# Suffix sums of a stick-breaking attention: fp32 products against fp32r products of a rounded part and an exact rest

## What is computed

```python
def block(args):
    qb, start = args
    z = jnp.einsum('bhqd,bhkd->bhqk', qb, k).astype(f32) * scale
    qpos = start + jnp.arange(Q_BLOCK)
    mask = kpos[None, :] < qpos[:, None]
    log_beta = jax.nn.log_sigmoid(z)
    log_1m = jnp.where(mask, jax.nn.log_sigmoid(-z), 0.0)
    between = lax.cumsum(log_1m, axis=3, reverse=True) - log_1m
    a = jnp.where(mask, jnp.exp(log_beta + between), 0.0)
    return jnp.einsum('bhqk,bhkd->bhqd', a.astype(v.dtype), v)
```

## Time and profile before

| | |
|---|---|
| three runs | 1589.37, 1589.56, 1590.39 us, median 1589.56 |
| profiled execution, first to last instruction (its span) | 1588.8 us |
| TensorE (PE) busy | 1560.3 us, 98% |
| weight loads (PEld), beside the products | 1402.7 us, 88% |
| VectorE (DVE) busy | 983.1 us, 62% |
| ScalarE (ACT) busy | 821.1 us, 52% |
| GpSimd (POOL) busy | 149.2 us, 9% |
| data moved | 309.40 MB |

### The profile page before, as it was taken

How to read it: one execution, slowest core, us unless ns; L and a number is a source line. 1 busy time by engine, 2 the same in 40 slices (tenths; PEclk the granted TensorE clock), 3 DMA queues, 4 the chain that set the end, 5 groups by cost and what they waited for, 6 DMA issues and landing times.

```text
span 1588.8 us, 25389 instructions
## 1 busy us (share of the span) xinstructions
PE 1560.3 (98%) x10689; PEld 1402.7 (88%) x10689; DVE 983.1 (62%) x1614; ACT 821.1 (52%) x1204; POOL 149.2 (9%) x140
## 2 busy tenths in 40 slices
PE   7999999999999999999999999999999999999997
PEld 6888999988989899997899999889888888889986
DVE  5786744446566664554765667568747866664554
ACT  4586544444579754453454564444545546364442
POOL 2220011000002101011001100001000000001000
PEclk9999999999999999999999999999999999999999
DMA  9766757766563476777555577599673565585552
GB/s 328 260 210 227 232 193 229 253 241 226 172 204 107 159 230 200 229 251 244 188 186 186 186 159 194 178 189 175 145 156 70 135 161 184 171 279 193 194 186 80
DMA packets 224418, 309.40 MB, mean 195 GB/s; under 512 B 5005, under 2 KB 146721, under 8 KB 224305
## 3 DMA queue, kind: packets, MB, share of 16 engines
q1 hardware_dynamic: 222208, 301.48, 62.3%
q0 software_dynamic: 1664, 5.84, 1.1%
q10 hardware_dynamic: 432, 0.45, 0.1%
HBM read 306.71 MB, written 1.05 MB: 194 GB/s over the span
## 4 chain that ended last, share of the span: by engine, by line
PE 88%; DVE 5%; ACT 5%; issue 1%; DMA 1%; POOL 0%; DVEq 0%; ACTq 0%
PE ps L137 86%; PE ps L140 3%; DVE wl L150 2%; ACT SA L146 1%; ACT L146 1%; ACT wh L146 1%; DVE SM L160 1%; ACT SA L147 1%; DMA raw<-in_a_w_qkv_dram 0%; DMA X<-in_x_dram 0%; DVE SA L160 0%; DVE X L160 0%; DVE FT L150 0%; DVE SM L157 0%; ACT OA L146 0%
## 5 line engine op out<-in xcount | busy, mean ns | idle before, releaser
L150 DVE TENSOR_TENSOR wl<-raw,wh 128x1024 fp32r<-128x1024 f32 x498 | 606.8, 1258 | 396.2 <-ACT wh L146 395.6
L146 ACT ACTIVATE wh<-raw 128x1024 fp32r<-128x1024 f32 x498 | 501.9, 1054 | 233.0 <-PE ps L137 117.0
L137 PE MATMUL ps<-XPf,wh 128*128 128x256 f32 x1408 | 242.6, 278 | 0.0
L137 PEld LDWEIGHTS ps<-XPf,wh 128*128 128x128 f32 x1408 | 212.7, 188 | 4.3 <-issue 4.2
L137 PE MATMUL ps<-XPf,wl 128*128 128x256 f32 x704 | 195.1, 277 | 0.0
L137 PE MATMUL ps<-XPc,wh 128*128 128x256 f32 x832 | 145.0, 279 | 0.0
L137 PE MATMUL ps<-wh,HTH 128*128 128x512 f32 x352 | 137.8, 392 | 0.0
L137 PE MATMUL ps<-wh,HTL 128*128 128x512 f32 x352 | 137.2, 390 | 0.0
L137 PE MATMUL ps<-wl,HTH 128*128 128x512 f32 x352 | 137.2, 390 | 0.0
L137 PEld LDWEIGHTS ps<-XPf,wl 128*128 128x128 f32 x704 | 132.3, 188 | 0.0
L137 PEld LDWEIGHTS ps<-XPc,wh 128*128 128x128 f32 x832 | 125.9, 188 | 1.2 <-issue 1.0
(11 more groups left out here) (350 smaller groups left out, 2704.0 us busy)
## 6 DMA issues: line engine op xcount, KB each, us to landing
raw<-in_w_ffn_in_dram SPq DMA_DIRECT2D x66, 1024.0 KB, 5.2
raw<-in_ffn_w_gate_up_dram SPq DMA_DIRECT2D x44, 1024.0 KB, 5.6
raw<-in_w_in_dram SPq DMA_DIRECT2D x40, 1024.0 KB, 8.6
raw<-in_w_ada_dram SPq DMA_DIRECT2D x36, 1024.0 KB, 5.2
raw<-in_w_ffn_out_dram SPq DMA_DIRECT2D x30, 1024.0 KB, 5.0
raw<-in_ffn_w_down_dram SPq DMA_DIRECT2D x20, 1024.0 KB, 5.1
raw<-in_a_w_qkv_dram SPq DMA_DIRECT2D x12, 1024.0 KB, 7.5
raw<-in_kv_w_dram SPq DMA_DIRECT2D x8, 1024.0 KB, 5.4
```

What stands on the lines that cost most here:

```text
L137: return NOTHING if self.e is None else self.e.matmul(o, l, r, start=start, stop=stop, skip_group_check=skip)
L146: return self.e.activation(o, i, fn, bias=bias, scale=scale)
L150: return NOTHING if self.e is None else self.e.tensor_tensor(o, a, b, f)
```

## The change

Phase 1 splits P, as the dense layers split their weights, and multiplies the parts as fp32r. ACT rounds P to fp32r (`high_parts`) into the free tile `SA[2*hd%8]`, seen there as `SAR[2*hd%8]`; DVE takes P minus it (`low_parts`) over P itself, `SAR[2*hd%8+1]`. TensorE multiplies constant by high part (384 columns, and 128 with `neg`), waits for the low part, and does the same with it. The constants stand as fp32r in `NEG` (written once, over a buffer `MT` that is free at that time). `high_parts` stands first in ACT's tick, `low_parts` first in DVE's, so both parts of a pair are made in the very tick in which TensorE multiplies them. The exponential of phase 1 no longer waits for DVE's "bp".

```diff
@@ -238,6 +238,7 @@
         C = fixed("C", [P, CK])
         SM = fixed("SM", [P, 208])
         MT = [fixed(f"MT{i}", [P, 512]) for i in range(2)]
+        NEG = at("NEG", [P, 2, P], fixed.o - 4096, F32R)
         FT = [fixed(f"FT{i}", [P, 512]) for i in range(2)]
         at0 = fixed.o
         AT = fixed("AT", [P, 512])
@@ -258,7 +259,9 @@
         kT = a_("kT", [P, 8, T])
         VA = a_("VA", [P, 2, D])
         OA = a_("OA", [P, 2, D])
+        sa0 = a_.o
         SA = [a_(f"SA{i}", [P, 384]) for i in range(8)]
+        SAR = [at(f"SAR{i}", [P, 384], sa0 + 1536 * i, F32R) for i in range(8)]
         TA = [SG[0], a_("TA1", [P, 384])]
         LV = at("LV", [P, 256], r0)
 
@@ -703,12 +706,15 @@
                     S, P_ = SA[2 * hd % 8], SA[2 * hd % 8 + 1]
                     if phase == 1:
                         o = ps("bs", hd)
-                        pe.wait_ge(*v_att.at("bm", hd))
-                        pe.wait_ge(*g_att.at("bm", hd))
-                        pe.mm(o[:, 0:256], con("ngt"), P_[:, 0:256], False, False, True)
-                        pe.mm(o[:, 128:256], con("neg"), P_[:, 256:384], False, True, True)
-                        pe.mm(o[:, 256:384], con("ngt"), P_[:, 256:384], False, True, True).then_inc(
-                            *scored.up("bb", hd))
+                        ngt, neg = NEG[:, 0, :], NEG[:, 1, :]
+                        high, low = SAR[2 * hd % 8], SAR[2 * hd % 8 + 1]
+                        pe.wait_ge(*a_small.at("neg"))
+                        pe.wait_ge(*a_att.at("bh", hd))
+                        pe.mm(o[:, 0:384], ngt, high[:, 0:384], False, False, True)
+                        pe.mm(o[:, 128:256], neg, high[:, 256:384], False, False, True)
+                        pe.wait_ge(*v_att.at("bl", hd))
+                        pe.mm(o[:, 0:384], ngt, low[:, 0:384], False, False, True)
+                        pe.mm(o[:, 128:256], neg, low[:, 256:384], False, True, True).then_inc(*scored.up("bb", hd))
                         give(("bs", hd), a_att, "ba", hd)
                 if phase == 2:
                     g, c0 = p // 2, T * (p % 2)
@@ -1362,7 +1368,6 @@
                     S = SA[2 * hd % 8]
                     if phase == 1:
                         act.wait_ge(*scored.at("bb", hd))
-                        act.wait_ge(*v_att.at("bp", hd))
                         act.act(S[:, :], ps("bs", hd)[:, 0:384], ACT.Exp).then_inc(*a_att.up("ba", hd))
                 if phase == 2 and p % 2:
                     g, H = p // 2, head("ho")
@@ -1375,6 +1380,12 @@
                     if g == 1:
                         act.wait_ge(*a_att.at("bo", 0))
                         act.act(H[:, 0:2, :], two(OA[:, 0, 0:512]), ACT.Copy).then_inc(*a_turned.up("ho", 0))
+
+            def high_parts(p):
+                for hd in (2 * p, 2 * p + 1):
+                    act.wait_ge(*v_att.at("bm", hd))
+                    act.wait_ge(*g_att.at("bm", hd))
+                    act.act(SAR[2 * hd % 8][:, :], SA[2 * hd % 8 + 1][:, :], ACT.Copy).then_inc(*a_att.up("bh", hd))
 
             def logarithms(p):
                 for hd in (2 * p, 2 * p + 1):
@@ -1521,10 +1532,15 @@
                         m = act.act(head("hq")[:, k, :], qT[:, k, :], ACT.Copy, 0.0, gain("mix_pre_g", 8)(k))
                     m.then_inc(*a_turned.up("hq", kp))
                 yield
+                act.act(NEG[:, :, :].rearrange("p a b -> p (a b)"), C[:, CC["ngt"][0]:CC["ngt"][0] + 2 * P], ACT.Copy
+                        ).then_inc(*a_small.up("neg"))
                 tick = iter(B_TICKS)
                 for step in B_STEPS:
                     if step == "t":
                         heads = next(tick)
+                        for p, phase in heads:
+                            if phase == 1:
+                                high_parts(p)
                         for p, phase in heads:
                             attention_b(p, phase)
                         for p, phase in heads:
@@ -1999,6 +2015,13 @@
                         dve.wait_ge(*a_att.at("ba", hd))
                         dve.tt(S[:, 0:128], S[:, 0:128], con("mlt"), ALU.mult).then_inc(*v_att.up("bw", hd))
 
+            def low_parts(p):
+                for hd in (2 * p, 2 * p + 1):
+                    i = 2 * hd % 8
+                    dve.wait_ge(*a_att.at("bh", hd))
+                    dve.wait_ge(*g_att.at("bm", hd))
+                    dve.tt(SAR[i + 1][:, :], SA[i + 1][:, :], SAR[i][:, :].bitcast(F32), ALU.subtract).then_inc(*v_att.up("bl", hd))
+
             def sizes(p):
                 for hd in (2 * p, 2 * p + 1):
                     dve.wait_ge(*scored.at("bs", hd))
@@ -2214,6 +2237,9 @@
                     if step == "t":
                         parts = next(tick)
                         for p, phase in parts:
+                            if phase == 1:
+                                low_parts(p)
+                        for p, phase in parts:
                             if phase == 0:
                                 sizes(p)
                         for p, phase in sorted(parts, key=lambda u: -u[1]):
```

## The result

| | before | after |
|---|---|---|
| median of four runs each | 1589.97 us | 1610.63 us |
| lowest to highest | 1589.37 to 1591.72 | 1610.11 to 1611.28 |
| ratio | | 1.0126, interval 1.0113 to 1.0140 |
| span of the profiled execution | 1588.8 us | 1609.5 us |
| mean granted clock of TensorE | 0.998 | 0.991 |

The change costs 20.7 us, 1.3%. The direction was forecast, the size was not: 12.7 us were forecast, and the range ended at 1607.

A forecast was written before the change was run, and what follows sets the result against it. With the added work, the loop of ACT and DVE was to outlast TensorE's period in the second attention: 10.7 us of delay plus 2.0 for the clock, +12.7 on 1589.6, giving 1602.3 us, range 1596 to 1607.

The forecast's parts named there:

- the walk of the prediction, without the clock: Second attention's eight ticks: TensorE waits for parts queued on DVE and ACT, 3.5 us late in the second, 10.7 by the eighth.
- the 0.76 us of slack: Second attention, kernel before: the loop of ACT and DVE takes 8.33 us against TensorE's period of 9.09.
- E: Start of ACT's first exponential in a tick of the second attention, put 0.58 us after DVE's sizes start.
- A: When ACT is free for a tick's high part: E + 5.9 us, plus any query copy, table load or gate.
- The clock: Second attention: TensorE's clock falls after gaps in the second and eighth ticks, 1.5 us a fall, together +2.0 us.
- My rival of three falls: Second attention: three clock falls of 3.0 us added to the 10.7 give 16.4, 1606 us; no chance of its own.
- The products' price: TensorE's 128-column fp32r products cost 0.06 us, at most 0.22; the new products save 0.87 us a tick, 7.0 in all.
- The first, products decide: Second attention: parts are ready before TensorE needs them, so its 7.0 us saving reaches the end: 1582.6 us, chance 5%.
- The second, a delay that comes once: Second attention: only the second tick costs 3.5 us, then gains and waits cancel: 1593.1 us, down to 1588; chance 9%.
- The third, the walk without the clock: Second attention: queue delays alone, 10.7 us, no clock fall: 1600.3 us; 84% together with the forecast.
- The fourth, fp32r as slow as fp32: Phase 1 products: fp32r pairs take 0.9 us instead of 0.23, 2.0 more by the eighth tick: 1604.3 us, chance 2%.
- What would show it: Trace signs in the second attention: some 14 us of waits for parts, 0.9 us products, eighth phase 1 ending near 538.

The follow-up runs named there:

- e5: The changed kernel plus 28, 7, 30 and 34 unread TensorE products filling its gaps in the second, fourth, sixth and eighth ticks: 1602.29 us, ratio 1.0080.
- e6: The kernel before, with P written directly as fp32r and multiplied once; no copies or subtractions, rest of P left out: 1590.73 us, ratio 1.0005.
- e1: The changed kernel, still making both parts, but TensorE multiplies whole P in fp32 as before and does not read them: 1598.51 us, ratio 1.0044.
- e2: The changed kernel plus 10 to 62 unread 128-column products per tick in TensorE's gaps, second to eighth tick: 1611.01 us, ratio 1.0122.

## Why the prediction was wrong in size

When TensorE moves on from each tick, as a delay against the kernel before (the stretch's own start, 0.7 us earlier in both traces, is taken out), in us:

| | T1 | T2 | T3 | T4 | T5 | T6 | T7 | T8 |
|---|---|---|---|---|---|---|---|---|
| the walk of the prediction, without the clock | 0.7 | 3.5 | 3.5 | 4.4 | 4.7 | 7.1 | 7.9 | 10.7 |
| e5, clock kept up | 0.9 | 3.7 | 3.7 | 4.5 | 4.8 | 7.8 | 8.5 | 11.9 |
| the change | 0.9 | 4.5 | 5.7 | 6.8 | 7.9 | 12.3 | 13.8 | 17.8 |

**What bounds the kernel.** The loop of ACT and DVE was the right thing to look at, but the 0.76 us of slack that I gave it isn't there. With it some 5 of the 7.3 us saved on TensorE in e6 should have come through, and none did. I had taken DVE's side of T3, 7.75 us, and added the 0.58 us from sizes to E as it is in T2. In T4 ACT is busy with a table load, a gate and another table load until 492.38, so E comes 1.36 us after sizes and 9.11 us after T3's. ACT's first exponentials of T4 to T7 in the kernel before:

```profile
492.39 0.94 ACT L146 ACTIVATE SA<-SA 128x384 f32<-128x384 f32 x2
...
501.03 0.94 ACT L146 ACTIVATE SA<-SA 128x384 f32<-128x384 f32 x2
...
511.40 0.94 ACT L146 ACTIVATE SA<-SA 128x384 f32<-128x384 f32 x2
...
520.95 0.94 ACT L146 ACTIVATE SA<-SA 128x384 f32<-128x384 f32 x2
```

From T2 (474.94) to T7 that is 46.01/5 = 9.20 us a tick, where TensorE leaves the same ticks 9.10 us apart (473.09 to 518.6). Over the stretch the loop is no shorter than TensorE's period, and at T8 TensorE's lead is used up: there it waits the 0.8 us of the earlier trace rows.

Of the 12.7 us by which e5 is slower than its own runs of the kernel before, 6.4 to 7.4 are the load (e1). The rest comes with the place: e5's 1602.3 less e1's 1598.5 is 3.8 us, and 5.3 with each taken against its own runs. It is only an estimate of that part, since e1 also has the slower fp32 products.

**The walk.** Right for seven ticks to 0.7 us, and 1.2 low at T8. Two things that it lacked would each push it up: TensorE's eight products take 1.20 us and not 0.91, and DVE's low part takes 0.8 us more in T6 and in T8. How much of either comes through wasn't tried by itself. Against e5 the walk's 10.7 us are 2.0 short of the 12.7 at the end of the program. Its own arithmetic slips by 0.2 us in T5 (A is 502.6 by its rule) and in T7 (524.8), which would have made T8 10.9.

**The clock: the step that failed.** I had +2.0 us in the sum; it is 8.0 to 8.3 (e5). Of the 8.0 us between the forecast's +12.7 and the measured +20.7, 6.0 are this term and 2.0 the walk. Three assumptions of the term fell.
1. *How many falls.* I looked for gaps longer than 2.8 us and counted T2 and T8. Four fills ran slowly, T4's and T6's among them, T4's after TensorE had stood 1.36 us in that tick.
2. *What one costs.* I took 1.5 us, the middle between 0 and 3.0. The fills lost 7.64 - 5.60 = 2.04, 1.60, 2.10 and 2.14 us. In T2, T6 and T8 the six products ahead of the fill were slow already, 1.65 or 1.66 us where e5 has 0.92 in T2 and 0.91 in T8, so a fall cost 2.8 to 2.9 us there, and 10.1 us all four. The Trainium skill (TensorE: Matmul & The Clock Gate, on HAM oscillation) would make each about 0.8 us, an estimate from its 1.67 us at the lower clock, half of it lost; this trace has two to three and a half times that, and the measurement decides.
3. *What of it goes on.* I let 0.5 us of T2's fall through, because ACT and DVE would be late anyhow. But ACT's high part of T3 stands behind a query copy that reads what the slow fill makes (2.60 us of waiting for TensorE at 484.60), so TensorE's slowness comes back to it through ACT. T5 and T7 have the same shape, and in e5 ACT waits for TensorE in none of the three. What doesn't go on is the time that TensorE would have stood anyway: in e5 it waits 0.59 us in T3, 0.71 in T5 and 1.04 in T7, 2.3 in all, and in the change not at all in these ticks. 10.1 less 2.3 is 7.8, close to the 8.0 to 8.3 measured. The delay grows by 2.0 us more than e5's until T3, and by 5.9 until T8.

The wait, then, costs twice: once while TensorE stands, once while it runs slowly afterwards; and the slow fill makes the next parts late, so that the loop doesn't catch up meanwhile. My rival of three falls, 1606, had the mechanism and was still too low, as it let two of three through at 1.5 and 1.2.

**The products' price.** I took 0.06 us for 128 columns against an upper end of 0.22; it is 0.112 (e2). With 1.20 us for a tick's eight products TensorE would gain 0.58 us a tick, not 0.87. It made little difference, as none of it was to come through.

**The rivals.** The first, products decide, 1582.6: e6 saves TensorE 7.3 us without any part to wait for and gains nothing. The Trainium skill says to optimize the busiest engine first (Perfetto Trace Analysis, Identifying the Most-Contended Engine). That isn't enough in this stretch: TensorE is the busiest engine, by its products (98%) and by its weight loads (88%), but it isn't the only one that binds. The second, a delay that comes once: the table shows it growing from T3 to T8. The third, the walk without the clock, 1600.3: e5, with the clock kept up, is at 1602.3. The fourth, fp32r as slow as fp32: 1.20 us for 2048 columns against 1.78 for 1024 before.

**What would show it.** As written: waits that name `tt`'s line and ACT's copy, the longest in T2, T6 and T8 (3.25, 3.17 and 3.51 us); dips of the clock; later stages of their old length. The sum of 14.2 us against "some 14" is luck in part. The walk has TensorE standing in T3, T5 and T7 too, where it doesn't stand in the change, as the slow fills used up that time; T6 and T8 have a second wait of 0.85 us each instead, for the low part. Not as written: the products take 1.20 us and not 0.9, phase 1 of T8 ends at 544.7 and not near 538, and ACT has idle time between T4 and T8 (1.32 us in T5, 2.57 and 0.60 in T6, 1.36 in T7).

## What to carry to other kernels

A stretch in which one engine is busy 98% of the time can be bound just as much by a loop of two others that answer each other. Before pricing what the busy engine would save, compare the loop's time with its period, over all rounds: the one round that I read had 0.76 us of slack by my sum, and the five rounds from T2 to T7 have none. Work that is added to such a loop delays the busy engine, whether that engine reads it or not. And a wait of TensorE is to be priced with what follows it: don't leave out gaps because they are shorter than those already seen to bring the clock down, take 2 to 3 us for a fall as measured here, and look at what the slowed products feed, since that comes back as the next wait; some useless products in the gap can be worth more than they cost.

## What was unexpected of the hardware

- **A fall of TensorE's clock after a short gap.** In T4 TensorE stood 1.36 us, after a T3 without a wait. The eight products behind the gap still ran at the full clock (1.00), and the fill behind them at a mean of 0.76. In e5, with seven products put into that gap and 92 into the three others, the same fill has 1.00. Which of the earlier gaps also counts there the runs don't tell.
- **POOL's subtraction holds DVE's up.** At 518.08 DVE's first low part takes 1.31 us in place of 0.55, while POOL's subtraction runs from 517.72 to 518.99; the second, after POOL has ended, takes its usual time. POOL's takes 1.27 us, no longer than in the kernel before (1.29). T8 is the same (1.79 us for DVE's pair). The Trainium skill (SBUF — State Buffer, Who interferes with whom) says that a DVE instruction with two inputs in SBUF and a GpSimd instruction that reads SBUF exclude each other, the later one waiting for the whole of the earlier. By that the first low part would end 0.55 us after 518.99, at 519.54. It ends at 519.39, so the trace agrees within 0.15 us.
- **An fp32r product of 128 columns costs as much as one of 256.** It takes 0.112 us (e2), and 256 columns take 0.113 (0.34 us for three). Each of e2's fifty products in T2 has a weight load of its own (the trace shows fifty); whether that sets the price wasn't tried.
